# A two-layer decoder trunk: gate and up with the weights stationary and the tokens moving

## What is computed

```python
D_MODEL = 2048; SEQ = 256; DEPTH = 2
D_FF = -(-8 * D_MODEL // (3 * 256)) * 256        # 5632
def _rmsnorm(x, w):
    y = xf * lax.rsqrt(jnp.mean(xf * xf, axis=-1, keepdims=True) + NORM_EPS)
    return (y * w.astype(jnp.float32)).astype(x.dtype)
def _swiglu(h, w_gate, w_up, w_down):
    return (jax.nn.silu(h @ w_gate) * (h @ w_up)) @ w_down
...
    h = _rmsnorm(x, norm_ffn[layer])
    x = x + _swiglu(h, *ffn[layer])
return _rmsnorm(x, final_norm)
```

## Time and profile before

| | |
|---|---|
| median of 3 runs | 2890.29 us (2888.48 to 2891.91) |
| the profiled execution, its own time | 2888.65 us |
| its span | 2886.9 us |
| granted TensorE clock, mean | 0.996 of 2.4 GHz |
| instructions in the span | 36757 |
| DMA | 502.66 MB, mean 174 GB/s |

### The profile page before, as it was taken

One profiled execution on the slowest core, in us unless ns is written; L12 is line 12 of the kernel. 1 busy time (PEld: TensorE's weight loads), 2 busy tenths in 40 slices (PEclk: granted clock), 3 DMA queues, 4 the chain that ended last, 5 costly groups with the idle time before them and its releaser, 6 DMA issues.

```text
span 2886.9 us, 36757 instructions
## 1 busy us (share of the span) xinstructions
PE 2817.2 (98%) x13396; PEld 2326.4 (81%) x13396; DVE 1561.2 (54%) x1934; ACT 1373.9 (48%) x1874; POOL 96.2 (3%) x67
## 2 busy tenths in 40 slices
PE   8999999999999999999999999999999999999998
PEld 6788788888888888887878787887888888888886
DVE  4554665544545455557585757655454454544444
ACT  5354545444444344455665657454444444444443
POOL 0000000000000000001010101000000000000000
PEclk9999999999999999999999999999999999999999
DMA  7464466666666666644353535555566666666664
GB/s 235 145 201 148 140 192 186 189 189 189 189 189 189 190 189 189 197 137 143 108 161 105 154 117 154 155 159 188 185 189 191 189 189 189 189 190 188 205 192 143
DMA packets 261264, 502.66 MB, mean 174 GB/s; under 512 B 20112, under 2 KB 20368, under 8 KB 260624
## 3 DMA queue, kind: packets, MB, share of 16 engines
q1 hardware_dynamic: 259504, 494.67, 57.3%
q10 hardware_dynamic: 816, 3.15, 0.3%
q0 software_dynamic: 816, 3.15, 0.3%
HBM read 495.65 MB, written 5.24 MB: 174 GB/s over the span
## 4 chain that ended last, share of the span: by engine, by line
PE 85%; DVE 7%; ACT 4%; issue 1%; DVEq 1%; ACTq 0%; DMA 0%; SPq 0%
PE acc L545 26%; PE acc L539 26%; PE acc L540 26%; PE aux L771 2%; DVE wlo L1397 2%; PE aux L592 2%; DVE const L1758 1%; DVE arena L1796 1%; ACT whi L967 1%; PE aux L780 1%; DVE arena L1793 1%; DVE arena L1758 1%; ACT arena L1313 0%; DVEq L1762 0%; PE aux L744 0%
## 5 line engine op out<-in xcount | busy, mean ns | idle before, releaser
L1397 DVE TENSOR_TENSOR wlo<-wraw,whi 128x1024 fp32r<-128x1024 f32 x928 | 1145.3, 1240 | 1142.3 <-ACT whi L967 1133.7
L967 ACT ACTIVATE whi<-wraw 128x1024 fp32r<-128x1024 f32 x928 | 973.7, 1060 | 1094.3 <-PE acc L545 1038.8
L539 PE MATMUL acc<-whi,hT_hi 128*128 128x512 f32 x2624 | 1040.0, 396 | 7.5 <-ACT whi L967 7.1
L540 PE MATMUL acc<-whi,hT_lo 128*128 128x512 f32 x2624 | 1024.4, 390 | 0.0
L545 PE MATMUL acc<-wlo,hT_hi 128*128 128x512 f32 x2624 | 708.5, 392 | 25.0 <-DVE wlo L1397 24.5
L545 PEld LDWEIGHTS acc<-wlo,hT_hi 128*128 128x128 f32 x2624 | 490.2, 188 | 142.9 <-DVE wlo L1397 42.0
L539 PEld LDWEIGHTS acc<-whi,hT_hi 128*128 128x128 f32 x2624 | 494.0, 188 | 109.4 <-issue 7.9
L540 PEld LDWEIGHTS acc<-whi,hT_lo 128*128 128x128 f32 x2624 | 494.1, 188 | 100.7 <-issue 1.0
L539 PE MATMUL acc<-whi,arena 128*128 128x512 f32 x1088 | 427.4, 393 | 3.2 <-ACT whi L967 3.2
L540 PE MATMUL acc<-whi,arena 128*128 128x512 f32 x1088 | 425.1, 391 | 0.0
L545 PE MATMUL acc<-wlo,arena 128*128 128x512 f32 x1088 | 293.4, 392 | 0.0
(11 more groups left out here) (234 smaller groups left out, 1191.0 us busy)
## 6 DMA issues: line engine op xcount, KB each, us to landing
wraw<-in_l_w_in SPq DMA_DIRECT2D x304, 512.0 KB, 3.8
wraw<-in_l_w_gate SPq DMA_DIRECT2D x176, 512.0 KB, 3.7
wraw<-in_l_w_up SPq DMA_DIRECT2D x176, 512.0 KB, 3.7
wraw<-in_l_w_down SPq DMA_DIRECT2D x176, 512.0 KB, 4.0
wraw<-in_l_w_out SPq DMA_DIRECT2D x96, 512.0 KB, 4.6
o_rounds<-arena POOLq DMA_DIRECT2D x3, 1024.0 KB, 4.7
arena<-o_rounds ACTq DMA_DIRECT2D x3, 1024.0 KB, 6.1
x<-in_x SPq DMA_DIRECT2D x4, 512.0 KB, 6.0
```

The costliest lines, as they stand in the source:

```text
L539: nc.tensor.matmul(pair[m], hi[:, k, tok], wh, start=first, stop=False)
L540: nc.tensor.matmul(pair[m], lo[:, k, tok], wh, start=False, stop=False)
L967: nc.scalar.activation(whi[:, s, :], wraw[:, s, :], ACT.Copy).then_inc(hi_done, 1)
L1397: V.tensor_tensor(wlo[:, s, :], wraw[:, s, :], whi[:, s, :].bitcast(F32), ALU.subtract).then_inc(lo_done, 1)
```

## The change

In the two FFN phases the operands change places. The stationary operand is a 128 x 128 piece of `whi` or `wlo`; what moves is `hT`. `hT_hi` and `hT_lo` become the two halves of one tensor `hT` [128, 16, 2, 256], so that one matmul moves 512 columns, 256 of hi and 256 of lo, and `wlo` is multiplied with the 256 columns of hi alone. A unit is then 8 matmuls of 512 columns and 8 of 256, in the order hi of the first k-tile, all of `wlo`, hi of the second. The result is channel-major: 4 banks a block, bank t holding 128 channels by [w x hi | w_hi x lo]. Gate blocks take the whole of the four `acc` banks, up blocks the four `aux` banks.

The two halves of a bank have to be added, and `rstd` is now a row along the tokens instead of a scalar: the first block makes it by a matmul of ones with `ident * rstd` (after unit 6) and VectorE copies it to SBUF. The transposes `tr` are gone, and `fT_hi`/`fT_lo` are split from `prod` in SBUF. PE's loop begins at trip 1 in place of 2.

```diff
@@ -185,8 +185,8 @@
-        hT_hi = sb("hT_hi", [P, KT, SEQ], F32R)
-        hT_lo = sb("hT_lo", [P, KT, SEQ], F32R)
+        hT = sb("hT", [P, KT, 2, SEQ], F32R)
+        hT_hi, hT_lo = hT[:, :, 0, :], hT[:, :, 1, :]
@@ -237,8 +237,10 @@
-        sg = at(88 * KB, [P, M, NB])
-        prod = xs
+        sg = at(88 * KB, [P, 4, SEQ])
+        prod = xs[:, :, :].rearrange("p m (e n) -> p (m e) n", n=SEQ)
+        row_r = C["decay"][:, 0:SEQ]
+        diag_r = C["decay"][:, SEQ:2 * SEQ]
@@ -283,8 +285,9 @@
-        acc = [ctx.enter_context(nc.psum_tensor(f"acc{i}", [P, M, NB], F32)) for i in range(2)]
-        aux = [ctx.enter_context(nc.psum_tensor(f"aux{i}", [P, 2 * NB], F32)) for i in range(2)]
+        banks = [ctx.enter_context(nc.psum_tensor(name, [P, 4, NB], F32)) for name in ("acc", "aux")]
+        acc = [banks[0][:, 2 * i:2 * i + 2, :] for i in range(2)]
+        aux = [banks[1][:, 2 * i:2 * i + 2, :].rearrange("p m n -> p (m n)") for i in range(2)]
@@ -565,6 +575,36 @@
                     if between is not None:
                         between(slot0 + j)
+            def channel_block(name, i, b, between=None):
+                upb = UPB[name]
+                base_u = i * (2 * upb) + (UNIT0[name] + b * upb)
+                first = isinstance(i, int) and i == 0
+                pe.wait_ge(acc_read[b], i + BLOCK0[name] // 2)
+                if first and b == 1:
+                    pe.wait_ge(row_set, BLOCK0[name] // BLOCK0["gu1"] + 1)
+                for j in range(upb):
+                    slot = (b * upb + j) % SLOTS
+                    weight = lambda w, kk, t: w[:, slot, kk * NB + t * P:kk * NB + (t + 1) * P]
+                    def hi_products(kk):
+                        k = 2 * j + kk
+                        for t in range(4):
+                            if first and b == 0 and k == 0 and t == 2:
+                                pe.wait_ge(acc_read[1], BLOCK0[name] // 2)
+                            mm = nc.tensor.matmul(banks[b][:, t, :], weight(whi, kk, t), hT[:, k, :, :].rearrange("p e n -> p (e n)"),
+                                                  start=k == 0, stop=k == KT - 1)
+                        return mm
+                    pe.wait_ge(hi_done, base_u + (j + 1))
+                    hi_products(0)
+                    pe.wait_ge(lo_done, base_u + (j + 1))
+                    for kk in range(2):
+                        for t in range(4):
+                            nc.tensor.matmul(banks[b][:, t, 0:SEQ], weight(wlo, kk, t), hT_hi[:, 2 * j + kk, :], start=False, stop=False)
+                    hi_products(1).then_inc(unit_used, 1)
+                    if between is not None:
+                        between(b * upb + j)
             def gate_products(layer):
                 pe.wait_ge(gw_lo_done, layer + 1)
...
@@ -630,18 +669,19 @@
                 return between
             def ffn(name, after, n0):
-                def tr(i):
-                    def f():
-                        pe.wait_ge(acc_read[1], i + BLOCK0[name] // 2)
-                        if n0 or not isinstance(i, int) or i > 1:
-                            pe.wait_ge(flo_done, i + (n0 - 1))
-                        transposes(prod_tile, aux[1], 4).then_inc(ft_ready, 1)
-                    return f
-                body(name, 0, 2, hT_hi, hT_lo, [None, None], between=last_x_block(after))
-                body(name, 1, 2, hT_hi, hT_lo, [tr(1), None])
-                with pe.Fori(2, FF // NB) as i:
-                    body(name, i, 2, hT_hi, hT_lo, [tr(i), None])
-                return tr(FF // NB), lambda w: pe.wait_ge(flo_done, n0 + FF // NB) if w == FKT // 2 - 3 else None
+                last_x = last_x_block(after)
+                def first(w):
+                    last_x(w)
+                    if w == 6:
+                        pe.wait_ge(row_diag, NORM_OF[after] // 2 + 1)
+                        nc.tensor.matmul(aux[1][:, 0:SEQ], C["ones"], diag_r, start=True, stop=True).then_inc(row_psum, 1)
+                for b in range(2):
+                    channel_block(name, 0, b, first)
+                with pe.Fori(1, FF // NB) as i:
+                    for b in range(2):
+                        channel_block(name, i, b)
+                return lambda w: pe.wait_ge(flo_done, n0 + FF // NB) if w == FKT // 2 - 3 else None
             def l0(name):
@@ -1026,11 +1066,19 @@
                 x_block(NORM_OF[name], 3, lambda m: xs[:, m, :])
             def ffn(name, after, n0):
+                def u_copy(i):
+                    act.wait_ge(unit_used, i * (2 * UPB[name]) + UNIT0[name])
+                    if isinstance(i, int) and i == 1:
+                        act.wait_ge(xs_copied, 4 * NORM_OF[after])
+                    else:
+                        act.wait_ge(flo_done, i + (n0 - 1))
+                    nc.scalar.activation(prod, banks[1][:, :, SEQ:], ACT.Copy).then_inc(u_part, 1)
                 def f_hi(i):
-                    act.wait_ge(ft_ready, i + n0)
-                    nc.scalar.activation(fT_hi[:, bass.ds(i * 4 - 4, 4), :].rearrange("p a b -> p (a b)"), aux[1][:, :], ACT.Copy
-                                         ).then_inc(fhi_done, 1)
+                    act.wait_ge(f_set, i + n0)
+                    nc.scalar.activation(fT_hi[:, bass.ds(i * 4 - 4, 4), :], prod, ACT.Copy).then_inc(fhi_done, 1)
                 def hook(i, b, j):
                     first = isinstance(i, int) and i == 0
@@ -1039,15 +1087,28 @@
                     if first and b == 0 and j == 4:
                         root(NORM_OF[after])
                     if b == 1 and j == 3:
-                        if not (first and n0 == 0):
-                            act.wait_ge(acc_read[1], i + BLOCK0[name] // 2)
-                        copy_out(name, i * 2, 0, lambda m: sg[:, m, :], ACT.Silu)
-                    if b == 0 and j == 7 and not first:
+                        act.wait_ge(unit_used, i * (2 * UPB[name]) + (UNIT0[name] + UPB[name]))
+                        if not first:
+                            act.wait_ge(f_set, i + n0)
+                        nc.scalar.activation(sg[:], banks[0][:, :, SEQ:], ACT.Copy).then_inc(g_part, 1)
+                    if b == 1 and j == 6:
+                        act.wait_ge(g_scaled, i + (n0 + 1))
+                        nc.scalar.activation(sg[:], sg[:], ACT.Silu).then_inc(g_silu, 1)
+                    if b == 0 and j == 3 and not first:
+                        u_copy(i)
+                    if b == 0 and j == 6 and not first:
                         f_hi(i)
                 body(name, 0, 2, hook)
-                with act.Fori(1, FF // NB) as i:
+                body(name, 1, 2, hook)
+                with act.Fori(2, FF // NB) as i:
                     body(name, i, 2, hook)
-                return lambda j: f_hi(FF // NB) if j == 7 else None
+                def last_f(j):
+                    if j == 3:
+                        u_copy(FF // NB)
+                    if j == 6:
+                        f_hi(FF // NB)
+                return last_f
             act.wait_ge(first_in, 16 * 2)
@@ -1461,34 +1522,60 @@
             def ffn(name, after, last_x_block, n0):
                 norm = NORM_OF[after]
+                rows = row_r.unsqueeze(1).to_broadcast([P, 4, SEQ])
+                def rstd_diag():
+                    for m in range(M):
+                        a = V.tensor_scalar(diag_r[:, m * P:(m + 1) * P], ident, rstd[:, m:m + 1], None, ALU.mult)
+                    a.then_inc(row_diag, 1)
+                def rstd_row():
+                    dve.wait_ge(row_psum, norm // 2 + 1)
+                    V.tensor_copy(row_r, aux[1][:, 0:SEQ]).then_inc(row_set, 1)
+                def gate_in(i):
+                    dve.wait_ge(g_part, i + (n0 + 1))
+                    V.tensor_tensor(sg[:], banks[0][:, :, 0:SEQ], sg[:], ALU.add).then_inc(acc_read[0], 1)
+                    dve.drain()
+                    V.tensor_tensor(sg[:], sg[:], rows, ALU.mult).then_inc(g_scaled, 1)
+                def gate_scaled(i):
+                    dve.wait_ge(g_silu, i + (n0 + 1))
+                    V.tensor_tensor(sg[:], sg[:], rows, ALU.mult)
                 def up(i):
-                    dve.wait_ge(acc_read[0], i + BLOCK0[name] // 2)
-                    dve.wait_ge(unit_used, i * (2 * UPB[name]) + UNIT0[name])
-                    if isinstance(i, int) and i == 1:
-                        dve.wait_ge(xs_copied, 4 * norm)
-                    else:
-                        dve.wait_ge(ft_ready, i + (n0 - 1))
-                    for m in range(M):
-                        a = V.scalar_tensor_tensor(prod[:, m, :], acc[1][:, m, :], rstd[:, m:m + 1], sg[:, m, :],
-                                                   op0=ALU.mult, op1=ALU.mult)
-                    a.then_inc(acc_read[1], 1)
+                    dve.wait_ge(u_part, i + n0)
+                    V.tensor_tensor(prod, banks[1][:, :, 0:SEQ], prod, ALU.add).then_inc(acc_read[1], 1)
```

(31 more changed lines are left out.)

## The result

The changed kernel takes **2898.83 us** (median of 7 runs, 2897.9 to 2901.65) beside 2891.44 for the kernel before (7 runs, 2888.48 to 2892.71). The ratio is 1.003, with a 95% interval from 1.0018 to 1.0042: slower by some 0.3%, or 7.4 us. The forecast was 2882.6, and faster. The profiled execution took 2898.66 with a span of 2896.9; the span before was 2886.9, so the two profiled executions stand 10.0 us apart.

What follows compares the result with a forecast made beforehand. PE's own stream was taken to bound the kernel. The terms -19.6 + 9.2 + 2.1 + 0.6 = -7.7 us gave a forecast median of 2882.6 us, with a range from 2868 to 2899, the instruction fetch left out.

Steps and rivals of the forecast that it cites:

- What bounds the kernel: Whole kernel, read in the FFN: PE's own stream bounds, so time changed there reaches the end one to one.
- The transposes, -19.6 us: FFN loop: removing 22 groups of `prod` transposes, none hidden, at 0.89 us each saves 19.6 us.
- The eight matmuls of 256 columns, p = 116.6 ns and +9.2 us: `wlo` part of each FFN unit: start-to-start distance p of 116.6 ns adds 26 ns a unit, +9.2 us over 352.
- given back: Rival, FFN units: load width raises p to 120.3 (2893 us), or the 512s cost 228.9 (2888.8); chance 0.28.
- The 512s, no change: `whi` part of each FFN unit: 512-column matmuls stay at 226.7 ns; other end 228.9 ns, +6.2 us.
- The entering wait, +2.1: Start of each FFN: PE's third matmul waits 1.0 to 1.1 us for the last residual add, +2.1 us.
- ones x diag, +0.6: First block of each FFN: one added fp32 matmul of 256 columns a layer, 0.3 us each, +0.6 us.
- Other engines, queues: VectorE, ScalarE and SyncE in the FFN: `wlo` and `whi` stay ready in time despite added work, charged at nothing.
- the instruction fetch: Rival, PE's loop: 512 recorded instructions a trip may not stay on chip, +67 us, near 2949; chance 0.04.
- The "slower" rival: `wlo` part of each unit: 128-wide loads no longer hidden, p 121.4, +5.7 us in all, 2896; chance 0.14.

Runs made afterwards that it cites:

- The last experiment but one: The kernel before with 2 of the 8 transposes in each of 22 groups, three quarters of the turned product left out: 2874.09 us, 14.7 less.
- the narrow-load experiment: The changed kernel with `wlo` matmuls loading 64 columns instead of 128, half of the w_lo x h_hi product left out: 2883.65 us.
- The long-stream experiment: The changed kernel with `wlo` matmuls moving all 512 columns, h_lo too, which adds a term w_lo x h_lo: 3195.15 us.
- The old kernel with short streams: The kernel before with each 512-column FFN gate and up matmul on `wlo` split into two of 256, transposes kept: 2916.58 us, +24.7.
- the two kernels in turns: The changed kernel alternating 512-column `whi` and 256-column `wlo` matmuls: 2891.73 us; the second also fills two banks before the FFN's entering wait: 2891.25 us.
- the twos: The changed kernel with two 512-column `whi` matmuls, then two 256-column `wlo` matmuls, four times a unit: 2899.26 us.

## Why the prediction was wrong

**What bounds the kernel: right.** PE waits once in each FFN and otherwise for nobody, and what its stream gained in length came out at the end (the sum below).

**The transposes, -19.6 us: right.** The last experiment but one measured 0.111 us for each, which for 176 is 19.6. The trips of the kernel before give a little more: nine of them between the starts of the first and the tenth group take 399.9 us, 144 units of 2.720 are 391.7, and the rest is 0.91 a group, 20.0 for 22.

**The eight matmuls of 256 columns, p = 116.6 ns and +9.2 us: this step failed.** Measured are 119.1 on average and 120 in the steady run, so 45.8 ns a unit against 26, and 352 x 45.8 ns = **+16.1 us**. The nearest row by type, operand and columns was the 64-wide gate load. It differed in the load's width, and with it in the partitions written, and the narrow-load experiment, which sets both to that row's 64, brings the same place to 113.3. The forecast took a rate for 64-wide loads and put the step to 128-wide ones at nothing. The other row that was weighed for a gain, L771 at 111.5, is of another type, and did not carry over to these. The estimate written down under "given back", 120.3 by the growth from 8 to 64 to 128 wide, hits the steady value, but by luck: in its picture a 64-wide load costs 3.2 ns, and in the runs of eight it costs nothing over the stream. The two rates that it took for a cost by width, 113.4 and 116.6, can't be that alone, since 8-wide loads ran at both the earlier trace rows; what parts them no run here shows.

**The 512s, no change: this failed too.** They were given 226.7 with 228.9 as the other end, for the place of the operand. The long-stream experiment shows 226.7 in the new place: the reason for which a change was feared is empty. But behind the run of 256s they take 27.5 ns a unit more, 352 x 27.5 = **+9.7 us**, above even the other end's 6.2. No rival named it: I priced each kind of matmul for itself, and not the passage from one to the other. The kernel before had the sequence already, with no 256-column stream near. Here it stands behind a wait of PE for `whi`, with 512s on both sides:

```profile
122.33 0.84 PE L545 MATMUL acc<-wlo,hT_hi 128*128 128x512 f32 x3
123.52 0.50 PE L539 MATMUL acc<-whi,hT_hi 128*128 128x512 f32 x1 [0.35 <-ACT whi L967]
123.86 0.40 PE L540 MATMUL acc<-whi,hT_lo 128*128 128x512 f32 x1
...
125.01 0.39 PE L539 MATMUL acc<-whi,hT_hi 128*128 128x512 f32 x1
```

From 123.86 on its distances are 235 229 232 231 227, and behind a group of four fp32 matmuls of 128 columns (L680, to 217.93) they are 314 236 228 233 231 and then 226. The 236 228 233 231 stands in some 150 places of that trace. So the late 512s are no property of the 256s: they follow other breaks in a stream of 512s too, and the changed kernel breaks it once in every unit. (The unit behind a transpose group, with its 2.82 for 2.72, shows less of it: distances of 314 233 231 226, in which the 314 is mostly the last transpose's own time.)

**The entering wait, +2.1: right.** The first FFN's start in the changed kernel's timeline, beside the earlier trace rows:

```profile
467.64 0.63 PE L595 MATMUL acc<-hT,whi 128*128 128x512 f32 x2
469.12 0.73 PE L595 MATMUL acc<-hT,whi 128*128 128x512 f32 x2 [0.85 <-DVE xs L1496]
469.68 1.11 PE L603 MATMUL acc<-hT,wlo 128*128 128x256 f32 x8
```

The third matmul starts at 469.12 and not at 467.64 + 0.46 = 468.10, so PE's stream stands for 1.0 us, of which 0.85 are shown as idle. The add (467.84 for 1.23) ends at 469.07, so the place and the cause are as forecast. The two matmuls from 469.12 to 469.68 take another 0.1 more than two in a running stream (335 and 233 ns), so it is 1.1 a layer, 2.3 for both.

**ones x diag, +0.6: right in kind.** In the first layer the profile shows it as two records:

```profile
489.21 0.59 PE L678 MATMUL aux<-const 128*128 128x256 f32 x2
489.45 1.28 PE L595 MATMUL acc<-hT,whi 128*128 128x512 f32 x4
490.56 0.63 PE L603 MATMUL acc<-hT,wlo 128*128 128x256 f32 x4
```

The next 512 starts 0.24 behind it, but that one takes 420 ns and not some 230, and the three behind it are late too. Together it is 0.45, so 0.9 for both layers.

**Other engines, queues and the instruction fetch: right.** VectorE's busy time over the FFN window rose from 251.09 to 296.73 us and it was never late; the instruction queue of the changed kernel from 560 to 960 us moves 2 packets on q14 and none on q8:

```profile
q1 hardware_dynamic: 38906, 75.00, 64.1%
q14 instruction: 2, 0.02, 0.0%
```

So nothing was fetched from trip to trip on q8, and the 142 units between 563.18 and 959.84 hold no wait at the loop's head: that rival (0.04) falls.

**The sum anew.** -20.0 + 16.1 + 9.7 + 2.3 + 0.9 = +9.0 us for the two FFNs. Measured from PE's first matmul of each stage to that of the next, the two gate and up stages grew from 488.7 to 494.1, 5.4 us each, and the two down projections lost 0.9 each, the transposes at their head: **+8.9**. The rest of the 10.0 lies where the change did nothing. In layer 1's output projection PE stands 3.15 us for the first `whi` in both kernels. Then come 12 matmuls on it, in the kernel before:

```profile
1984.97 0.50 PE L539 MATMUL acc<-whi,arena 128*128 128x512 f32 x1 [3.15 <-ACT whi L967]
...
1987.84 0.39 PE L539 MATMUL acc<-whi,arena 128*128 128x512 f32 x1
```

and in the changed one:

```profile
1988.96 0.50 PE L549 MATMUL acc<-whi,arena 128*128 128x512 f32 x1 [3.15 <-ACT whi L1007]
...
1993.41 0.40 PE L549 MATMUL acc<-whi,arena 128*128 128x512 f32 x1
```

They take 2.87 and 4.45 us. The windows behind the wait (columns as in the earlier trace rows) have a granted clock of 1.00 and of 0.76, first of the kernel before, then of the changed one:

```profile
1985.00:1992.00 7.00, 7.00 (x31) 5.75 (x32) 7.00 (x7) 3.83 (x4) 0.00 (x0) 1.00 0.47 149
```

```profile
1989.00:1996.00 7.00, 7.00 (x24) 5.59 (x25) 7.00 (x7) 3.80 (x4) 0.00 (x0) 0.76 0.46 147
```

The changed kernel ran a part of these matmuls at 1.2 GHz, the other not: +1.6, and with -0.3 over the rest of layer 1's mixer and -0.1 ahead of the first FFN the 10.0 are placed. The old kernel with short streams, the narrow loads and the fewer transposes show this stage at its old length, the long streams and the two kernels in turns at +1.6, and the twos at +3.2, so it goes by no count of the changed work. Whether it belongs to a kernel or to an execution, one profile of each can't say. The distance of the medians, 7.4, is less than that of the spans: the profiled execution of the kernel before was 2.8 under its median in the later runs, and that of the changed kernel 0.2.

The prediction said that the total is zero at p = 119.4 with the 512s unchanged. On p alone (119.1) the change would have stayed a gain of 1 us, inside what can be told from none; the 9.7 of the 512s turned it into a loss. The "slower" rival's 2896 was near in time. Its mechanism, a 128-column load that a 256-column stream doesn't hide, is the reading that fits the larger part of the loss, at 120 and not at its 121.4. The other part is a cost that no case held, so that the time came near is in part luck.

**The rule that spoke against the change.** The measured pitch behind 256 columns is 120 ns with 128-wide loads and 113.3 with 64-wide ones. The Trainium skill ("TensorE: Matmul & The Clock Gate", LDWEIGHTS) lets a load take its columns / 1.2 ns, an estimated 107 for 128 columns and 53 for 64. The direction agrees, since only the 128-wide loads show. The size does not: 107 would still fit under the stream's 113.3, and the measured pitch is 120. What the load adds to come out there no run here shows.

## What to carry to other kernels

Before a stream of N columns is cut in two to save other work on TensorE, ask whether the weight load still hides behind the half: here matmuls with 128-wide loads ran at 226.7 ns for 512 columns, and at 120 in place of 113.3 for 256. Price the order too, since short and long streams in one unit are not the sum of their own rates: eight short ones in a run made a unit 2.793 us, the same sixteen in turns 2.773. Look in the old trace for what a stream loses after any break in it, start to start, before you put new breaks into a loop of 352 units. And when the nearest row differs from the new operation in just one thing, take that thing's whole plausible cost as the forecast's width, above all where 3 ns decide the sign.

## What the hardware showed unexpectedly

- Long streams behind short ones are late for some five matmuls: 233, 236, 228, 233 and 231 ns, then 227. It is the same with 64-wide and 128-wide loads in the short part, and with either operand stationary. The kernel before shows the same sequence behind a wait of PE and behind fp32 matmuls, so it follows a break in the stream of 512s and not short streams alone. Its cause was not found.
- In strict turns the excess found with 128-wide loads, 6.7 ns a pair, is split between both, at 230 and 117.
- Behind one and the same stall of 3.15 us the clock fell to its lower level in some kernels and not in others, which moved 1.6 to 3.2 us between kernels with the same work there.
- The first short distance behind a long stream is 113 even with 128-wide loads, the second 119, then 120, as if the load ran ahead a little and were caught up. With 64-wide loads it goes the other way, 118 and 117 and then 113.3.
- In L603's records a 128-wide load lasts 187 or 188 ns behind a long stream and at the start of a run of short ones, and 192 in the rest of the run. That is longer than the 120 between two of them, so load records overlap, and their duration is no measure of what a load costs.
